# A two-block network kernel on one core: the opening transfers reordered, the gates' projection ahead of the memory's entry, two expert parts parked in a free buffer, fewer fillers

## The reference

```
x = x + concat(sliding_window_attention, mlstm)(rms_norm(x) @ w_in) @ w_out   # w_in: q, k, v | q,k of mlstm | v, o | 8 gate columns
x = x + cross_attention(rms_norm(x), rms_norm(mem)) @ w_co                    # mem: 256 rows, w_cq, w_ckv
x = x + moe(rms_norm(x))          # 32 experts 1024->512->1024, 4 groups, top 2 of 8 in the chosen group
x = rms_norm(x)
# second block: ffn, attention with selected keys, ffn | ffn, gated mlp, ffn | rms_norm
```

## Time and profile before

| | us |
|---|---|
| median of three runs (1876.67 to 1879.33) | 1878.82 |
| the profiled execution | 1880.42 |
| its span, first to last instruction | 1878.6 |
| TensorE busy in the span | 1799.0 (96%) |
| DVE / ACT / POOL busy | 1293.8 / 1033.1 / 107.7 |
| mean granted clock | 0.984 |

### The profile page before, as it was taken

How to read it: one execution, slowest core, us unless ns; L and a number is a source line. 1 busy time by engine, 2 the same in 40 slices (tenths; PEclk the granted TensorE clock), 3 DMA queues, 4 the chain that set the end, 5 groups by cost and what they waited for, 6 DMA issues and landing times.

```text
span 1878.6 us, 22423 instructions
## 1 busy us (share of the span) xinstructions
PE 1799.0 (96%) x9232; PEld 1521.2 (81%) x9232; DVE 1293.8 (69%) x1285; ACT 1033.1 (55%) x1068; POOL 107.7 (6%) x106
## 2 busy tenths in 40 slices
PE   7999699999999998999999899999999999999998
PEld 6987578888788877788889788887888789878886
DVE  4776589999999998655458655545554668755553
ACT  4554478898888896544343354435443544434442
POOL 2101111010101000000010000000000100000000
PEclk8999899999999999999999999999999999999999
DMA  9734389999999999555564255555555654446551
GB/s 316 244 132 157 113 314 408 408 418 413 408 409 415 408 405 371 219 180 181 180 226 160 90 189 181 180 200 182 188 179 200 226 196 163 160 169 206 193 180 45
DMA packets 70174, 451.53 MB, mean 240 GB/s; under 512 B 11385, under 2 KB 11877, under 8 KB 18736
## 3 DMA queue, kind: packets, MB, share of 16 engines
q1 hardware_dynamic: 59184, 423.87, 60.2%
q0 software_dynamic: 10672, 25.60, 4.4%
q10 hardware_dynamic: 208, 0.54, 0.1%
HBM read 450.07 MB, written 14.16 MB: 247 GB/s over the span
## 4 chain that ended last, share of the span: by engine, by line
PE 75%; DVE 9%; DMA 9%; ACT 4%; issue 2%; POOL 0%; SPq 0%; ACTq 0%; POOLq 0%; DVEq 0%
PE PS L453 21%; PE PS L455 20%; PE PS L454 20%; DMA ring<-in_wt 7%; PE PS L1501 6%; DVE wl L434 5%; PE PS L1507 2%; ACT wh L425 2%; PE PS L2089 1%; DMA gmem<-in_norm_mem 1%; PE PS L1492 1%; ACT yr L1833 1%; PE PS L2596 1%; DVE xg__150 L507 1%; DMA y_d<-yr,ints 1%
## 5 line engine op out<-in xcount | busy, mean ns | idle before, releaser
L434 DVE TENSOR_TENSOR wl<-ring,wh 128x2048 fp32r<-128x2048 f32 x355 | 804.6, 2273 | 323.6 <-ACT wh L425 321.5
L425 ACT ACTIVATE wh<-ring 128x2048 fp32r<-128x2048 f32 x355 | 672.6, 1903 | 353.8 <-PE PS L455 307.6
L453 PE MATMUL PS<-wh,XTh 128*128 128x512 f32 x952 | 378.7, 398 | 14.2 <-DVE wl L434 8.6
L455 PE MATMUL PS<-wh,XTl 128*128 128x512 f32 x952 | 371.8, 391 | 0.0
L454 PE MATMUL PS<-wl,XTh 128*128 128x512 f32 x952 | 371.4, 390 | 0.0
L453 PEld LDWEIGHTS PS<-wh,XTh 128*128 128x128 f32 x952 | 179.3, 188 | 54.9 <-DVE wl L434 12.1
L455 PEld LDWEIGHTS PS<-wh,XTl 128*128 128x128 f32 x952 | 179.0, 188 | 38.3
L454 PEld LDWEIGHTS PS<-wl,XTh 128*128 128x128 f32 x952 | 179.3, 188 | 35.4 <-issue 0.2
L1501 PE MATMUL PS<-wh,xgT 128*128 128x512 f32 x384 | 155.1, 404 | 0.7 <-DVE xgT L1694 0.7
L1501 PE MATMUL PS<-wl,xgT 128*128 128x512 f32 x384 | 150.9, 393 | 0.0
L453 PE MATMUL PS<-XTh,wh 128*128 128x256 f32 (+2 forms) x480 | 137.6, 287 | 1.5 <-DVE wl L434 1.5
(11 more groups left out here) (438 smaller groups left out, 2533.7 us busy)
## 6 DMA issues: line engine op xcount, KB each, us to landing
ring<-in_wt SPq DMA_DIRECT2D x399, 1024.0 KB
xtmp<-in_norm_g POOLq DMA_DIRECT2D x6, 512.0 KB, 5.4
toep<-frow POOLq DMA_DIRECT2D x1, 2048.0 KB, 50.7
y_d<-in_zero POOLq DMA_DIRECT2D x1, 2048.0 KB, 26.1
yy<-y_d POOLq DMA_DIRECT2D x4, 512.0 KB, 5.3
bv<-in_b_b_in POOLq DMA_DIRECT2D x1, 1536.0 KB, 10.9
ring<-in_wt SPq DMA_DIRECT2D x2, 528.0 KB
X<-in_x SPq DMA_DIRECT2D x2, 512.0 KB, 6.8
```

The source lines that it names most:

```text
L425: s.activation(k.pieces(i)[0], k.raw(i), ACT.Copy).then_inc(*k.w_hi.up(i))
L434: v.tensor_tensor(l, k.raw(i), h.bitcast(F32), ALU.subtract).then_inc(*k.w_lo.up(i))
L453: pe.matmul(o, lhsT=left[0], rhs=right[0], start=first, stop=False)
L455: return pe.matmul(o, lhsT=left[1], rhs=right[0], start=False, stop=final)
```

## The change

- SP's opening order: x half 0, the identity, parts 0 and 1 in halves, x half 1, part 2, the constants `iota` and `ones`, part 3, `gmem`, `mem`, part 4, the other constants, part 5 and on. `mem` and `gmem` are no longer POOL's.
- ACT and DVE split part 1 in halves too, and each half of t = 0's entry just ahead of the half that needs it; TensorE's first products follow (`opening`), and the 6 fillers become 4.
- TensorE: part 2 stands ahead of the first half of the memory's entry, and the products for it move to the place after `rb1` in DVE's order. Part 3 stands between the halves.
- Part 6's first two column groups stand ahead of the scores, the other two behind; the crow products wait for `cst`.
- Parts moe+6 and moe+7 land in `XT` (`park`), loaded once `lg` is done; `turn` counts the ring's slots without them, so each load from moe+8 to moe+12 waits for a split two places earlier than otherwise. SP issues two more parts ahead of the branch.
- The 10 fillers ahead of the first gathered tokens go; the 3 behind them stay.

```diff
 def load_part(sp, k, i):
     if i >= len(k.parts):
         return
+    if i in k.parked:
+        park_part(sp, k, i)
+        return
     if i >= RING:
-        sp.wait_ge(*k.w_lo.at(i - RING))
-    sp.dma_start(k.raw(i), k.part_in(i)).then_inc(*k.d_w[i % RING].up(i))
+        past = i - RING
+        if i > k.parked[1] and past - 2 < k.parked[0]:
+            past -= 2
+        sp.wait_ge(*k.w_lo.at(past))
+    sp.dma_start(k.raw(i), k.part_in(i)).then_inc(*k.landing(i).up(i))
+
+def park_part(sp, k, i):
+    sp.wait_ge(*k.moe.pe.at("lg"))
+    sp.dma_start(k.raw(i), k.part_in(i)).then_inc(*k.landing(i).up(i))
...
     enter_tensor(pe, k, m, 0, 0, k.xs1)
-    warm(pe, k, k.warm, k.warm, 7, 6)
+    warm(pe, k, k.warm, k.warm, 7, 4)
     i = k.at["in"]
-    first_rows(pe, k, m, i, 0, k.xs1)
+    pe.wait_ge(*m.v.at("xl0.0"))
+    pe.wait_ge(*k.w_lo.at("half0"))
+    opening(0, 0, 2)
+    pe.wait_ge(*k.w_lo.at(0))
+    opening(0, 2, 4)
+    pe.wait_ge(*m.v.at("xl0.1"))
+    pe.wait_ge(*k.w_lo.at("half1"))
+    opening(0, 4, 6)
+    enter_tensor(pe, k, m, 1, 0, k.xs1)
+    pe.wait_ge(*k.w_lo.at(1))
+    opening(0, 6, 8)
+    for p in T:
+        pe.wait_ge(*m.v.at(f"xl1.{p}"))
+        opening(1, 4 * p, 4 * p + 4).then_inc(*k.w_used.up(i + p))
...
+    rows_part(pe, k, i + 2, XT, 0, 2, C_JOBS)
     enter_tensor(pe, k, M, 0, MEM_BANKS, k.memg)
-    rows_part(pe, k, i + 2, XT, 0, 2, C_JOBS)
+    rows_part(pe, k, i + 3, XT, 1, 2, C_JOBS)
     pe.wait_ge(*M.v.at("xl0.1"))
     enter_tensor(pe, k, M, 1, MEM_BANKS, k.memg)
-    rows_part(pe, k, i + 3, XT, 1, 2, C_JOBS)
...
+    vg, l0 = m.v.at("gi"), m.v.at("L0")
+    columns_part(pe, k, m, i + 6, 0, XT, (2, 3, 0, 1), "qm", (vg, vg, l0, l0), (0, 1))
     pe.wait_ge(*m.v.at("q3"))
     pe.wait_ge(*m.v.at("kT"))
     scores(0)
     scores(1)
-    vg, l0 = m.v.at("gi"), m.v.at("L0")
-    columns_part(pe, k, m, i + 6, 0, XT, (2, 3, 0, 1), "qm", (vg, vg, l0, l0))
+    columns_part(pe, k, m, i + 6, 0, XT, (2, 3, 0, 1), "qm", (vg, vg, l0, l0), (2, 3))
...
     scaled(0)
-    enter_low(v, k, m, 0, 0)
-    split_first_lo(v, k)
+    enter_low(v, k, m, 0, 0, None, (0,))
+    for x in T:
+        split_half_lo(v, k, 0, x)
+    enter_low(v, k, m, 0, 0, None, (1,))
+    split_half_lo(v, k, 1, 0)
     scaled(1)
-    split_lo(v, k, 1)
+    split_half_lo(v, k, 1, 1)
     enter_low(v, k, m, 1, 0)
+    split_lo(v, k, 2)
     for t in T:
         enter_mean(v, k, m, t)
-    split_lo(v, k, 2)
...
-    for t in T:
-        for nn in T:
-            enter_gain(v, k, M, t, nn, k.d["mem"].at("mem"), k.d["gmem"].at("gmem"), k.gmem, k.memg, k.mem)
     split_lo(v, k, k.after[i])
     v.wait_ge(*m.pe.at("gc"))
     v.tensor_copy(k.gcol[:, 0:40], bank(7, 40)).then_inc(*m.v.up("gc"))
     split_lo(v, k, k.after[i + 1])
     v.wait_ge(*m.pe.at("rb"))
     v.tensor_copy(k.rb1, bank(3, 256)).then_inc(*m.v.up("rb"))
+    for t in T:
+        for nn in T:
+            enter_gain(v, k, M, t, nn, k.d["mem"].at("mem"), k.d["gmem"].at("gmem"), k.gmem, k.memg, k.mem)
...
-    g.wait_ge(*k.d_w[1].at(1))
-    g.dma_start(k.mem, a["mem"][0].rearrange("(t p) n -> p t n", p=128)).then_inc(*k.d["mem"].up("mem"))
-    g.dma_start(k.gmem, a["norm_mem"].broadcast_to([128, 1024])).then_inc(*k.d["gmem"].up("gmem"))
...
-    warm(pe, k, k.ones, k.upper[:, 0, 0:128], 3, 10)
     turn_x(0)
     warm(pe, k, k.ones, k.upper[:, 0, 0:128], 3, 3)
```

More of the change, by code:

```diff
@@ L208 @@
 STAGES = ("first", "memory", "cross", "moe", "f0", "A", "f1", "f2", "B", "f3", "end")
-LANDINGS = ("ident", "cst", "rows", "x0", "x1", "rel", "mem", "b", "toep", "sel", "gmix", "gmem", "ga", "gl", "gc", "late", "gf", "gn", "wr", "xn", "zero", "yy", "bt", "ki",
-            "wsp", "bsp", "bcol", "bv", "gain", "out", "w0", "w_half", "w1", "w2", "w3", "w4", "xg0", "xg1", "xz", "yd0", "yd1",
+LANDINGS = ("ident", "cst", "rows", "x0", "x1", "rel", "ones", "mem", "b", "toep", "sel", "gmix", "gmem", "ga", "gl", "gc", "late", "gf", "gn", "wr", "xn", "zero", "yy", "bt", "ki",
+            "wsp", "bsp", "bcol", "bv", "gain", "out", "w0", "half0", "half1", "park0", "park1", "w1", "w2", "w3", "w4", "xg0", "xg1", "xz", "yd0", "yd1",
             "rest_xg", "rest_w", "rest_yd")
@@ L231, in __init__ @@
         self.d = {n: make("d_" + n, 16) for n in LANDINGS}
-        self.d_w = [self.d[f"w{i}"] for i in range(RING)]
         self.parts, self.at = weight_parts()
+        self.parked = [self.at["moe"] + RING + 1 + x for x in T]
         self.part_at = [0] + list(itertools.accumulate(128 * nk * w for nk, w, _ in self.parts))
@@ L385, in col, with turn, landing @@
         return self.gcol[:, o:o + n]
+    def turn(self, i):
+        return i if i < self.parked[0] else i - 2
     def raw(self, i):
-        return self.ring[:, i % RING, 0:self.parts[i][0] * self.parts[i][1]]
+        n = self.parts[i][0] * self.parts[i][1]
+        if i in self.parked:
+            return self.park[:, i - self.parked[0], 0:n]
+        return self.ring[:, self.turn(i) % RING, 0:n]
+    def landing(self, i):
+        if i in self.parked:
+            return self.d[f"park{i - self.parked[0]}"]
+        return self.d[f"w{self.turn(i) % RING}"]
     def part_in(self, i):
@@ L508, in enter_gain, with enter_high @@
                     (k.gain if gain is None else gain)[:, o:o + 512], ALU.mult).then_inc(*m.v.up(f"xg{t}.{nn}"))
-def enter_high(s, k, m, t, h, xt=None):
-    for nn in T:
+def enter_high(s, k, m, t, h, xt=None, halves=T):
+    for nn in halves:
         s.wait_ge(*m.pe.at(f"xt{t}.{nn}"))
@@ L567, in first_rows @@
         if t == 0:
[L568 removed]
+            pe.wait_ge(*k.w_lo.at(i + p))
         pe.wait_ge(*m.v.at(f"xl{t}.{p}"))
@@ L645, in rows_part, with columns_part @@
     mm.then_inc(*k.w_used.up(i))
-def columns_part(pe, k, m, i, p, xt, banks, name, past):
+def columns_part(pe, k, m, i, p, xt, banks, name, past, some=range(4)):
     pe.wait_ge(*k.w_lo.at(i))
     w = k.weights(i)
-    for c in range(4):
+    for c in some:
         if p == 0:
@@ L1240, in first_scalar @@
     i = k.at["in"]
-    enter_high(s, k, m, 0, 0)
-    split_first_hi(s, k)
-    split_hi(s, k, 1)
+    enter_high(s, k, m, 0, 0, None, (0,))
+    for x in T:
+        split_half_hi(s, k, 0, x)
+    enter_high(s, k, m, 0, 0, None, (1,))
+    for x in T:
+        split_half_hi(s, k, 1, x)
     enter_high(s, k, m, 1, 0)
@@ L2896, in sync_program @@
     first_sync(sp, k)
-    ahead = k.at["moe"] + SPLIT + RING
+    ahead = k.at["moe"] + SPLIT + RING + 2
     for i in range(k.at["moe"], ahead):
```

60 lines of the change are left out of this document (35 added, 25 removed).

## The result

The changed kernel takes 1869.88 us (median; 1865.46 to 1873.43), the kernel before 1879.05 us beside it (1876.67 to 1880.94). The ratio is 0.9948 with a 95% interval from 0.9933 to 0.9964: faster by 6.8 to 12.6 us. The forecast was 1861.3 us in a range from 1856 to 1870, so the sign was right and the gain is about half of the 17.5 us that the sum had. The time lies 0.12 us inside the slow end of the range, much less than two medians of one kernel differ by: that it fell inside is luck.

A forecast was written before the change was run, and what follows sets the result against it. Loads were taken to bound the experts and TensorE the rest. Opening 11.5 plus experts 6.0 (2.0 + 4.5 - 0.5) gave 17.5 us: 1862.9 on the trace, 1861.3 for the median, range 1856 to 1870.

The forecast's parts named there:

- What bounds the kernel: Whole kernel: loads bound the experts, TensorE the rest; DVE bounds 260:290; in 290:718 DMA share 1.01, TensorE slack 9.9 us.
- First products: Opening: part 1 ahead of x half 1 and split in halves starts TensorE's products sooner, gaining 3.0 us (2.0 to 3.3).
- ACT waiting for a landing in the opening: Sign of a wrong forecast: ScalarE stands waiting for a load to land in the opening.
- the gather 2.3 us later behind `lg`: Sign of a wrong forecast, before the experts: the gather comes later behind `lg` by over 1.5 us.
- the same waits for the ring from 300 us on: Sign of a wrong forecast, in the experts: waits for the ring from 300 us on stay the same.
- Memory's entry: Opening: early `gmem` and `mem` and part 2 ahead remove the 6.7 us `gcol` wait and slow clock; 7.45 us (5.5 to 8.45).
- scores: Attention scores: two column groups ahead cover the 2.07 us wait; turn 1.65 us sooner, less 0.6: 1.05 (-0.7 to 2.7).
- The opening together: Opening up to 73 us: the gains 3.0, 7.45 and 1.05 sum to 11.5 us.
- Fillers: Ahead of the first gate: without 10 fillers TensorE turns the tokens at once, partly at slow clock; 2.0 us (0.4 to 3.1).
- Parking: Experts: loads two parts ahead gain 4.5 us (0.5 to 6.2); sharing engines with `xn_d` costs 0.5 (0 to 1.5).
- Rival 1: Experts: DVE's bound start and TensorE's order eat the loads' lead, only the fillers' 2 us stay; 1865.8 us, chance 0.15.
- Rival 4: Opening: parts 5 to 8 land late beside `toep` and `alibi`, making the kernel slower; 1882 us, chance 0.02.

The follow-up runs named there:

- late broadcasts: Changed kernel with GpSimd's four small broadcast loads (`sink`, `bgate`, `brg`, `bre`) moved behind the load of `attg`: 1864.92 us, ratio 0.9915 to the kernel before.

## Why the prediction was right in its sign and twice too large

**What bounds the kernel.** Right: the opening and the first gate gave time one for one, and both kept it to the end (12.8 us at the first gate, 12.8 at split 40).

**First products, 3.0 forecast.** -1.5 in the kernel after, +3.1 with the broadcasts out of the way (first product 1.0 us sooner, the wait of 2.1 gone). The walk through ScalarE and VectorE was right, though its parts as written, 0.7 + 2.1 - 0.3, give 2.5 and not 3.0; the step that failed is "part 1 now stands ahead of x half 1 (at 411 GB/s ...)". It took the rate of the opening as given and listed what SP's queue carries, but not what GpSimd issues once its wait is gone. This one omission cost 4.6 us: 2.7 of the second wait, 1.7 of the lower clock behind it, 0.2 of the first wait. What was written as a sign of error, "ACT waiting for a landing in the opening", is exactly what the trace shows. Two more of these signs came, too: the gather 2.3 us later behind `lg`, and the same waits for the ring from 300 us on.

**Memory's entry, 7.45, and scores, 1.05.** From the transpose to the turn the kernel before takes 46.27 us, after 36.99: 9.3 sooner. The forecast had 7.45 and 1.65 at that point, 9.1. Its `memg` wait was to be 1.0 and is 0.7; the scores' own share came out as 1.2. The sizes were right. Within the entry's term the credit was not: I gave it to the order of both, and it is the early transfers', all but 0.3 us.

**The opening together.** 11.5 forecast; 12.4 with late broadcasts, 7.8 in the kernel after. The further 2.9 us up to `xn_d` are the slow stretch of the clock in the profiled execution of before, which the prediction had named as chance with 1.75; they are probably most of what the trace gained (12.8 us) over the medians (9.2).

**Fillers, 2.0 (0.4 to 3.1).** 2.2 where the kernel after is compared with itself, 3.3 in the kernel before. The size was right: the turn then starts some 3.5 us behind the gather, as worked out. I had charged 2.7 us of gates at half rate; in this execution of the kernel after there were none, in seven of the eleven executions without the fillers there were some. (The bounds were worked out loosely: 4.1 less half of 2.7 us is 2.8, not 3.0, and less half of 6.2 us is 1.0, not 0.4.) By the rule of the Trainium skill ("TensorE: Matmul & The Clock Gate", part 1 and "PE-mode transpose") the ten fillers end the slow stretch and the term would have been 0.4. The trace agrees in part: with the fillers the gate started at 1.00 in both executions, without them in four of eleven. But the size is not 0.4, since the slow clock cost 1.1 us of the 4.4 in the kernel before and nothing of the 2.2 in the kernel after; there the measurement decides.

**Parking, 4.5, less 0.5 for `xn_d`.** 0, and a cost of 2.3 (9.47 - 7.14). This is the second failed step and the larger in itself. The sentence that fails is "It is worth that only if TensorE and DVE follow: TensorE's slack of 9.9 us in 290:718 allows it". The slack lies at the wrong place: the parked parts can be spent only while they are there, from the first gate to about 260 us, and in 240:260 VectorE had 0.04 us to give and TensorE 0.00 (0.86 where the parks came behind the gather). After that the stock of loaded parts is bounded by the ring again. The rival said so ("a full ring", 29.90 of 30 us) and had 0.15 of the chance; it deserved most. For the cost, I compared sums of bytes (4.7 MB by 232.5) and not the landing of the one transfer that the gather waits for: 8.6 us in place of 5.4, behind 3.1 MB (zeros and parked parts) issued in the 5 us ahead of it.

The account for the traces: 7.8 (opening) + 2.9 (clock) - 2.3 (`xn_d`) + 4.4 (gather to first gate) = 12.8. Forecast, in the same order: 11.5, 0, -0.5, 2.0, and 4.5 of parking behind it. The last two of the measured terms hang together: the 4.4 are those of a gather on time, and with the later gather the fillers' removal is worth 2.2 in all.

**The rivals.** Rival 1 is what happened in the experts. Rival 4 had the right kind of mechanism, an opening load that comes late, but the wrong loads and the wrong place (parts 5 to 8 at 45 us, where nothing was late). No rival named GpSimd's small loads.

**A better kernel.** The changed kernel with late broadcasts takes 1864.92 us, some 5 us under the changed kernel. Without parking it takes 1864.66; of the two equal ones this is the simpler.

## What to carry to other kernels

Whoever takes a wait out of a queue releases everything queued behind it, not only the instruction that it stood in front of: list those, the small ones too, and ask what they share with the loads that the start waits for. Stock laid in ahead of a stage is worth time only if, while the stock lasts, some engine behind it was waiting for loads; read the busy share of all consumers in the stretch in which the stock would be used, not in the long stretch behind it. A transfer whose bytes fit into a gap can still delay the single small transfer that the critical chain waits for: put it behind that one's landing, or check the landing and not the sum.

## What the runs showed of the hardware that I had not expected

- **A few packets of small broadcast loads hold the DMA engines.** 109 packets with 0.02 MB held 39.3% of 16 engines for 4 us, nearly all of it in 22 packets of 128 and 256 B that took 0.18 to 1.81 us each, while the core's rate was 167 GB/s over 7:11 in place of 412. The same loads do so wherever they lie: 299 GB/s in 34:38 in place of 417. 26 KB of them cost 4.6 us at the start of this kernel. The Trainium skill ("DMA: Bandwidth & Descriptors", "Why small descriptors are slow") gives each small packet an overhead of a few cycles and 32 B of metadata; that rule points the same way but is far too small for 1 us a packet, and the trace's packets of the same size with 0.02 us don't follow it.
- **Loads in another queue delay a write that the chain waits for.** The write of `xn_d` took 8.6 us in place of 5.4 with two parked parts (2.1 MB) issued 5 us ahead of it in another queue; the gather's small landing behind two parks took 7.75 us to the turn in place of 3.70.
- **Slow stretches of the clock with TensorE busy throughout** (0.60 in 112:118 of before, 0.83 and 0.88 in 100:112 of the kernel with late broadcasts and no parking) differ from execution to execution of nearly the same program and move a trace by up to 3 us. In all seven that have one between 101 and 120 us, it began 2 to 4 us after the start of eight small products on 4 rows (`crow`), with six of 4 columns behind them; in the other seven the same products ran and the clock stayed at 1.00. What decides between them stays open. A term of that size can be read off milestones of two traces only from the point where it acts to the next, never from the ends of the spans.
